# Alternating wide and narrow fp32r matmuls in the long phases of a two-block transformer layer, with one wide matmul per stretch read and written in runs of two columns

## What is computed

```python
# first block
xn = rms_norm(x, g);  proj = xn @ w_in                   # 2048 -> 4104 + 4*2048
y_a, y_b, y_c, y_d = lru(..), pool(..), shortconv(..), attention(..)
x = x + (sum_k sigmoid(gate_k) * (y_k @ w_branch[k])) @ w_out
x = x + relu(rms_norm(x, g) @ w_mlp_up)**2 @ w_mlp_down  # 2048 -> 8192 -> 2048
# second block
proj = rmsnorm(h, g) @ w_in_2
ya, yb = dilated attention @ w_branch_a, stick-breaking attention @ w_branch_b
h = h + rmsnorm((gate_a * ya + gate_b * yb) @ w_out_2, g)
up = conv3(rmsnorm(h, g) @ w_up_2)                       # 2048 -> 2 * 5632
h = h + rmsnorm((gelu(gate_ff) * value) @ w_down_2, g)
h = h + sigmoid(h @ w_ple_gate_2) * (p @ w_ple_in_2)
```

## Time and profile before

| | |
|---|---|
| Time, median of 3 runs | 2929.5 us (2927.82 to 2929.56) |
| The profiled execution, its own time | 2927.94 us |
| its span, first to last instruction | 2925.5 us |
| PE busy | 2914.1 us (100%), 17276 matmuls |
| PEld busy | 2567.7 us (88%) |
| DVE busy | 1925.1 us (66%) |
| ACT busy | 1511.0 us (52%) |
| DMA, mean | 187 GB/s |
| Granted TensorE clock, mean | 1.000 |

### The profile page before, as it was taken

One profiled execution on the slowest core, in us unless ns is written; L12 is line 12 of the kernel. 1 busy time (PEld: TensorE's weight loads), 2 busy tenths in 40 slices (PEclk: granted clock), 3 DMA queues, 4 the chain that ended last, 5 costly groups with the idle time before them and its releaser, 6 DMA issues. The chain is left out here.

```text
span 2925.5 us, 48783 instructions
## 1 busy us (share of the span) xinstructions
PE 2914.1 (100%) x17276; PEld 2567.7 (88%) x17276; DVE 1925.1 (66%) x2213; ACT 1511.0 (52%) x1896; POOL 229.5 (8%) x193
## 2 busy tenths in 40 slices
PE   9999999999999999999999999999999999999999
PEld 8888898998888888888888888988888888888888
DVE  6696765566665656656656666655887567757775
ACT  5576644455544444444544446555665455545564
POOL 1010020102101010000200000001000000010021
PEclk9999999999999999999999999999999999999999
DMA  8566657665565656656565555556465666656545
GB/s 255 165 180 185 169 183 228 188 178 190 191 194 184 196 187 186 194 182 197 181 194 183 167 161 167 186 184 208 154 212 179 196 189 188 191 187 188 186 158 172
DMA packets 543862, 545.95 MB, mean 187 GB/s; under 512 B 17304, under 2 KB 542112, under 8 KB 543744
## 3 DMA queue, kind: packets, MB, share of 16 engines
q1 hardware_dynamic: 540576, 536.79, 59.4%
q0 software_dynamic: 2480, 7.10, 0.9%
q10 hardware_dynamic: 688, 0.53, 0.1%
HBM read 542.25 MB, written 2.11 MB: 186 GB/s over the span
## 5 line engine op out<-in xcount | busy, mean ns | idle before, releaser
L1648 DVE TENSOR_TENSOR w_low<-raw,w_high 128x1024 fp32r<-128x1024 f32 x1012 | 1262.8, 1261 | 773.1 <-ACT w_high L1081 768.2
L1081 ACT CAST w_high<-raw 128x1024 fp32r<-128x1024 f32 x1012 | 1050.4, 1049 | 992.0 <-PE ps_gemm L704 965.1
L699 PE MATMUL ps_gemm<-act_a,w_high 128*128 128x512 f32 x4448 | 1433.6, 395 | 4.4 <-DVE act_a L2206 1.8
L699 PE MATMUL ps_gemm<-act_b,w_high 128*128 128x512 f32 x3208 | 1044.3, 395 | 0.0
L704 PEld LDWEIGHTS ps_gemm<-act_a,w_low 128*128 128x128 f32 x4608 | 861.7, 188 | 152.0
L704 PE MATMUL ps_gemm<-act_a,w_low 128*128 128x256 f32 x4608 | 991.8, 279 | 0.0
L704 PE MATMUL ps_gemm<-act_b,w_low 128*128 128x256 f32 x3520 | 778.8, 279 | 0.0
L699 PEld LDWEIGHTS ps_gemm<-act_a,w_high 128*128 128x128 f32 x4448 | 713.1, 188 | 50.5 <-issue 5.3
L704 PEld LDWEIGHTS ps_gemm<-act_b,w_low 128*128 128x128 f32 x3520 | 652.5, 189 | 96.9
L699 PEld LDWEIGHTS ps_gemm<-act_b,w_high 128*128 128x128 f32 x3208 | 524.4, 188 | 42.4
L1718 DVE TENSOR_TENSOR summ<-ps_gemm,bcopy 128x512 f32<-128x512 f32 x218 | 149.1, 684 | 8.8 <-ACT bcopy L1096 8.7
(11 more groups left out here) (290 smaller groups left out, 1235.9 us busy)
## 6 DMA issues: line engine op xcount, KB each, us to landing
raw<-in_w_in SPq DMA_DIRECT2D x348, 512.0 KB, 4.4
raw<-in_w_up SPq DMA_DIRECT2D x176, 512.0 KB, 3.5
raw<-in_w_mlp_up SPq DMA_DIRECT2D x128, 512.0 KB, 3.9
raw<-in_w_mlp_down SPq DMA_DIRECT2D x128, 512.0 KB, 3.5
raw<-in_w_down SPq DMA_DIRECT2D x88, 512.0 KB, 3.4
raw<-in_w_out SPq DMA_DIRECT2D x64, 512.0 KB, 4.6
raw<-in_w_branch SPq DMA_DIRECT2D x32, 512.0 KB, 3.5
raw<-in_w_ple_gate SPq DMA_DIRECT2D x32, 512.0 KB, 3.4
```

The costliest lines, as they stand in the source:

```text
L699: nc.tensor.matmul(ps[:, g, t, :], wh[:, at, o:o + P], x, start=first, stop=False, skip_group_check=True)
L1081: nc.scalar.copy(wh[:, at, :], raw[:, at, :]).then_inc(high_ready, 1)
L1648: nc.vector.tensor_tensor(wl[:, at, :], raw[:, at, :], wh[:, at, :].bitcast(F32), ALU.subtract).then_inc(split_done, 1)
```

## The change

Fifteen phases are named in `ALTERNATE`; their pieces, where not folded, now go wide, narrow, wide, narrow like those of the mlp. These are 32 + 32 + 32 + 32 + 4 + 32 pieces (proj_a, gates_a2, gates_a3, slots0, slots0_end, gates_b1) and 56 + 32 + 64 + 32 + 48 + 12 + 9 + 16 + 4 (ffn_up0 to ple_gate_end), 437 in all.

Eight of these phases are also in `IN_TURN`. In each, one piece of the first body (unit and piece given: the piece behind the sum of squares in proj_a, slots0 and ffn_up0, the phase's first in the others) has its very first wide matmul issued with another order of columns: two of the high half, the matching two of the low half, the next two of the high half, and so on, for reads of `x` and for writes of the bank alike. The same products land in the same places. In the five of them that had no body written out (gates_a2, gates_a3, gates_b1, ffn_up1, ple_gate) the first body now stands ahead of the loop.

```diff
--- before.py
+++ after.py
@@ -110,6 +110,12 @@
     "squared": {"resid": [1, 1], "mix": [1, 1], "accsq": [1, 1, 1, 1]},
     "sq_added": {"resid": [1, 1], "mix": [1, 1], "accsq": [1, 1, 1, 1]},
 }
+
+
+ALTERNATE = {"proj_a", "gates_a2", "gates_a3", "slots0", "slots0_end", "gates_b1", "ffn_up0", "ffn_down0", "ffn_up1",
+             "ffn_down1", "ffn_up2", "ffn_down2", "ffn_down2_end", "ple_gate", "ple_gate_end"}
+IN_TURN = {"proj_a": (0, 3), "gates_a2": (0, 0), "gates_a3": (0, 0), "slots0": (1, 0), "gates_b1": (0, 0),
+           "ffn_up0": (0, 3), "ffn_up1": (0, 0), "ple_gate": (0, 0)}
 
 
 def folded(ph, j):
@@ -668,7 +674,7 @@
             def high(t):
                 return t[:, 0:S]
 
-            def piece(ph, x_in, need, i, j, s, need_tile=None):
+            def piece(ph, x_in, need, i, j, s, need_tile=None, in_turn=False):
 
                 n, g, at = unit_no(ph, i, j), bank(ph, j), slot(ph, j, s)
                 if s == 0:
@@ -695,6 +701,10 @@
                                              start=first, stop=False, skip_group_check=True)
                             nc.tensor.matmul(ps[:, g, t, 0:S], wh[:, at, o:o + P], x[:, S:2 * S],
                                              start=False, stop=False, skip_group_check=True)
+                        elif k == t == 0 and in_turn:
+                            nc.tensor.matmul(ps[:, g, t, :].rearrange("p (e c r) -> p c e r", e=2, r=2),
+                                             wh[:, at, o:o + P], x.rearrange("p (e c r) -> p c e r", e=2, r=2),
+                                             start=first, stop=False, skip_group_check=True)
                         else:
                             nc.tensor.matmul(ps[:, g, t, :], wh[:, at, o:o + P], x,
                                              start=first, stop=False, skip_group_check=True)
@@ -703,7 +713,7 @@
                         o = k * S + t * P
                         return nc.tensor.matmul(ps[:, g, t, 0:S], wl[:, at, o:o + P], high(x),
                                                 start=False, stop=final, skip_group_check=True)
-                    if not ph.name.startswith("mlp_"):
+                    if folded(ph, j) or not (ph.name in ALTERNATE or ph.name.startswith("mlp_")):
                         high_product(0)
                         high_product(1)
                         low_product(0)
@@ -720,12 +730,14 @@
                     for j in range(ph.U):
                         for s in range(ph.ppu):
                             peeled = isinstance(i, int) and i == 0
-                            piece(ph, x_in, need, i, j, s, need_tile if peeled and j == 0 else None)
+                            piece(ph, x_in, need, i, j, s, need_tile if peeled and j == 0 else None,
+                                  peeled and IN_TURN.get(ph.name) == (j, s))
                             if once and peeled and (j, s) == at:
                                 once()
-                if once:
+                apart = once or ph.name in IN_TURN
+                if apart:
                     body(0)
-                over(pe, body, 1 if once else 0, ph.bodies)
+                over(pe, body, 1 if apart else 0, ph.bodies)
 
             def straight(phases):
 
```

## The result

The changed kernel takes 2933.14 us (median of 20 runs, 2931.65 to 2935.75) against 2929.18 (20 runs, 2927.68 to 2930.48): ratio 1.0015, interval 1.0009 to 1.0021. Forecast was 2924.4. The time lies in the range and within 0.2% of the kernel before, but the kernel became slower where a small gain was forecast. The profiled execution took 2933.29, its span 2930.8 against 2925.5.

The account below looks back on a forecast made before the run. TensorE, through the distances between matmul starts, was taken as the bound. 5.75 us gained less 0.23 at slow entries gave 5.5, less 0.4 for matmuls in turn 5.1: 2924.4 us against 2929.5, range 2922.5 to 2935.

Parts of the forecast that it names:

- (3): Eight matmuls in turn: 50 ns each, 0.4 us in all; any cost also makes a small jolt.
- a jolt gives the good pace: Entries to alternating stretches: a break in the flow, as behind mlp_up0's sum of squares, leads to 2.7733 us a piece.
- The three paces: TensorE's time a piece: grouped order 2.7867 us, alternating order 2.7733 us at its good pace, 2.8258 us at its slow one.
- (1): Order of 437 pieces, grouped to alternating: 5.83 us less at the good pace, 17.0 us more at the slow one.
- (2): Entries of proj_a and ffn_up0: three slow pieces each, 0.23 us lost, 5.5 us net; slots0's four pieces stay good.
- (4): Five first bodies ahead of their loops: more instructions to fetch, no wait or semaphore added, cost zero.
- (5): Supply by ScalarE and VectorE: cost zero; w_high next to be late, by 0.85 us at most without slack.
- Once in it nothing threw it out: Good pace in the mlp: held through all eight phases, loop ends, semaphores and epilogues included.
- C: Rival: slow rhythm in ffn_up0 with ffn_down0 and ffn_up1 to ffn_down2_end, 13.1 us for both, 2937.5 us; chance 0.15.
- B: Rival: matmul in turn gives no jolt; gates_a2, gates_a3, gates_b1 and ple_gate with its end slow, 2930.1 us; chance 0.17.
- D: Rival: the eight matmuls in turn are dear, 0.5 us each, 4.0 us instead of 0.4, 2928.0 us; chance 0.09.
- E: Rival: columns alone set the pace where epilogues differ from the mlp's, order gives nothing, 2929.5 us; chance 0.05.

Follow-up runs that it names:

- experiment 3: The kernel before with a matmul in turn as the first of mlp_down0 and of the six mlp phases behind it; one run, 2928.93 us.
- 7: The changed kernel with two more matmuls in turn, the first of ffn_down1 and of ffn_up2; one run, 2928.44 us.
- 9: The changed kernel with a matmul in turn as the first of ffn_down0 too; one run, 2926.94 us.
- experiment 8: The changed kernel with w_out and w_out2 phases alternating too, matmuls in turn only behind folded phases; 2923.39 us, ratio 0.9981 to the kernel before.
- 5: The changed kernel with ffn_up1's matmul in turn one k-tile later; one run, 2934.13 us.
- 6: The changed kernel run once more, nothing altered; one run, 2932.20 us.
- experiment 2: The changed kernel with no matmul in turn anywhere, the order of the 437 pieces kept; one run, 2929.03 us.
- experiment 4: The changed kernel with ffn_up1's first body still ahead of its loop but its first matmul plain; one run, 2926.28 us.
- experiment 1: The changed kernel without the matmuls in turn and written-out bodies of ffn_up1 and ple_gate; 2924.31 us, ratio 0.9985 to the kernel before.
- 10: The changed kernel with the first two k-tiles of ffn_up1 in turn instead of the first alone; one run, 2926.30 us.

## Why the prediction was wrong

The step that failed is the end of (3): that a matmul in turn, if it costs anything, is a small jolt and a jolt gives the good pace. It is a jolt, but what it gives depends on what it meets. By the runs: the one-pair cycle stays good (seven times in experiment 3, once in 7), the slow pace becomes good (7 and 9, one case each), a folded phase is followed by the good pace (three phases in each of eight executions, five entries in experiment 8), and the two-pair cycle becomes slow, in every execution that had one there and no second such matmul right behind (the changed kernel, 5, 6, 7 and 9), always at the same point of that cycle. Directly behind a sum of squares, in proj_a, slots0 and ffn_up0, the pace was good with it and, in 2 and 8, without it. ffn_down0 came out of ffn_up0 in the two-pair cycle in all of these, and in 2 and 8 too, where ffn_up0 has a sum of squares and no matmul in turn; so ffn_up1's matmul in turn spoiled a pace that needed no help. That cost 6.7 us over 165 pieces, where the prediction had a gain of 2.2. I had read one good cycle in the mlp and took it for the only one; a single jolt in the trace was the whole evidence for "a jolt gives the good pace", and I gave it 0.54.

The rest, by the prediction's own steps. The three paces were right in size: 2.7733 and 2.7867 as measured, slow 2.8274 against 2.8258. (1) Right as a price for each pace. (2) proj_a's entry was slow as taken; ffn_up0's was good in the changed kernel's trace and slow in others, by the half of the grouped cycle; slots0's four pieces kept the good one, as taken. (3) Cost of the matmul in turn: 0.09 to 0.13 us against 0.05 taken, within the bounds. (4) and (5) Right: no wait appeared, and experiment 4 clears the written-out body of ffn_up1; that of ple_gate was never tried alone. "Once in it nothing threw it out" was true of what the trace contained and was carried to an instruction it did not contain.

Of the rivals, C named the mechanism and one of its two stretches, ffn_up1 to ffn_down2_end: "a jolt of another size can end in either rhythm". With 185 slow pieces instead of the 250 it priced, the time lies short of the 210 from which the kernel counts as slower. B's premise, that a matmul in turn costs nothing and changes nothing, fell; its other half, that plain folded entries are slow, is what experiment 2 showed. D and E fell. The sum with the right signs would have been: 2929.2 + 6.7 (ffn_up1 to ffn_down2_end) + 0.9 (ple_gate) - 2.5 = 2934.3 against 2933.14 measured; in the traces, 2925.5 + 5.1 = 2930.6 against 2930.8. The medians' difference is of the size of the clock's 1.6 us and ple_gate's 1.0, which come and go between executions.

The rule in the Trainium skill, "Advanced Engine Details and Errata", section Memory Cachelines, by which runs of two values are enough in both memories, does not make such a matmul free here: 0.32 to 0.34 us to the next matmul instead of 0.23. Reads and writes were changed together in every run, so which of the two costs it is not shown.

## What to carry to other kernels

When a small reordering makes matmuls faster in one place, ask which stable rhythms the new order has and how each stretch enters its own, before multiplying the gain by the number of pieces: here one matmul decided over 165 pieces. A remedy for a bad entry belongs only where the entry is bad, since in a stretch that already runs well it is a risk of the same size. Read the distances of starts in ns over a few pairs, at the start and in the middle of every stretch, and not only their sum, for two rhythms of the same mean can answer differently to the same jolt.

## What the runs showed of the hardware that was not expected

An alternating sequence of a 512-column and a 256-column fp32r matmul, each with its own 128x128 weight load, ran in three stable cycles here, all at granted clock 1.00: 230, 117 ns; 231, 112, 233, 117 ns; and 232, 118, 240, 120, 236, 114 ns, the last 2% slower. They held through loop ends and semaphores, the first over 224 pieces (mlp_down0 to mlp_down3), the second over 197 (ffn_down0 to ffn_down2_end in experiment 1), the slow one over 165. What makes them was not found.

In seven of the profiled executions (1, 2, 4, 5, 7, 8, 10) the granted clock fell behind the norm ahead of ple_gate_0, in the others, before and after among them, it did not. Busy time in three stretches of experiment 8's kernel, then in two of the changed kernel (PE, PEld, DVE, ACT, POOL, clock, DMA share, GB/s):

```profile
2825.00:2828.00 3.00, 2.16 (x9) 1.94 (x10) 2.90 (x7) 2.23 (x5) 0.00 (x0) 0.82 0.00 0
2828.00:2831.00 3.00, 3.00 (x13) 2.55 (x12) 2.79 (x6) 1.24 (x2) 0.00 (x0) 0.62 0.00 0
2831.00:2834.00 3.00, 3.00 (x20) 2.60 (x19) 2.90 (x5) 2.25 (x3) 0.00 (x0) 1.00 0.01 3
```

```profile
2833.00:2836.00 3.00, 1.22 (x9) 1.00 (x8) 2.92 (x9) 1.83 (x5) 0.00 (x0) 1.00 0.09 31
2836.00:2840.00 4.00, 4.00 (x24) 3.48 (x24) 3.79 (x8) 2.54 (x5) 0.00 (x0) 1.00 0.00 0
```

TensorE had waited for the norm, 2.06 us from the start of its last matmul to that of ple_gate_0's first, and then worked for some 3 us at the lower level, 1.2 GHz (granted clock 0.50 from 2827 to 2830 in experiment 8's trace): the first piece of ple_gate_0 took 4.1 to 4.4 us instead of 2.86 to 2.87, and the phase as a whole 1.5 to 1.6 us more. In the changed kernel the wait was 2.06 us as well and the clock stayed at 1.00. What decides between the two was not found.

It is no matter of the change. Of the 15 runs of the kernel before beside experiment 1, the eight with a mean clock of 0.999 took 2929.26 to 2930.58 us, the seven with 1.000 took 2927.37 to 2928.72; beside experiment 8 it was three and twelve. Of the changed kernel's 20 runs, thirteen had 1.000. Both traces of the comparison have 1.000, and the median of the kernel before lies among its runs with 0.999. As far as such means can tell, that is why 5.3 us stand between the traces and 4.0 between the medians.

In experiment 1's trace the 1.2 us by which the expectation was missed are made up of 1.6 more in ple_gate_0 and 0.2 more in ffn_up0, which was entered slow, against 0.7 less in proj_0. None of this bears on a pace above, because each of them was read elsewhere, at clock 1.00.
